# Eight conditioning chunks computed inside the first attention instead of in the output projection and feed-forward

## The reference, cut to what matters

```python
# first block
proj = rms_norm(h, norm_mix) @ w_in                      # 3128 columns
h = h + concat([rwkv7_group(...), nsa_group(...)]) @ w_out
h = h + (silu(rms_norm(h, norm_ffn) @ w_gate) * (rms_norm(h, norm_ffn) @ w_up)) @ w_down
# second block, for l in range(2)
mod_x = silu(c) @ w_ada[l] + b_ada[l]                    # 9 x 1024 modulation values
mod_c = silu(c_ctx) @ w_ada[l] + b_ada[l]
h_x = _half_ffn(...); h_c = _half_ffn(...)               # use mod_x, mod_c, from here on
...
```

## Time and profile before

| | |
|---|---|
| median of 3 runs | 2290.67 us (2289.95 to 2290.98) |
| the profiled execution | 2294.01 us, of which the span 2292.6 us |
| PE busy | 2161.4 us (94% of the span) |
| DVE, ACT, POOL busy | 1078.5, 772.7, 51.8 us |
| chain of work that ended last, by engine | PE 84%, DVE 7%, ACT 5%, DMA 2% |
| granted TensorE clock, mean | 0.962 of full |
| first attention | about 231 to 276 us of the span |
| output projection, norm, feed-forward of the first block | about 276 to 547 us |

### The profile page before, as it was taken

The page is one execution under the profiler, slowest core; times in us unless marked ns, Lnnn a source line. Parts: engine busy times, 40 slices in busy tenths (PEclk is TensorE's granted clock), DMA queues, the critical chain, the costliest instruction groups (busy, mean ns, idle before and its releaser), DMA issues.

```text
span 2292.6 us, 40371 instructions
## 1 busy us (share of the span) xinstructions
PE 2161.4 (94%) x17742; PEld 1845.1 (80%) x17742; DVE 1078.5 (47%) x1613; ACT 772.7 (34%) x1094; POOL 51.8 (2%) x58
## 2 busy tenths in 40 slices
PE   7987789998999999998899999999999999999998
PEld 7886589997888788785578888887888887768997
DVE  5654555456333333557563333345333335765554
ACT  5321434344221222324632222223222323364443
POOL 0000020000000000031000000000000000200000
PEclk9998689998999999999999999999999999999999
DMA  7526146654345444531023232232223225304543
GB/s 274 194 78 254 42 184 231 256 193 148 129 161 213 188 170 176 159 95 56 1 92 129 69 124 92 77 110 87 91 93 111 86 78 137 113 1 147 177 176 106
DMA packets 56635, 303.70 MB, mean 132 GB/s; under 512 B 13728, under 2 KB 17184, under 8 KB 27552
## 3 DMA queue, kind: packets, MB, share of 16 engines
q1 hardware_dynamic: 56480, 301.40, 37.0%
HBM read 300.33 MB, written 1.05 MB: 131 GB/s over the span
## 4 chain that ended last, share of the span: by engine, by line
PE 84%; DVE 7%; ACT 5%; DMA 2%; issue 2%; SPq 0%; ACTq 0%; DVEq 0%
PE ps L448 22%; PE ps L449 21%; PE ps L450 21%; PE ps L548 3%; PE ps L549 3%; PE ps L552 3%; DVE w_lo L435 3%; PE ps L477 3%; ACT w_hi L429 2%; PE ps L1559 1%; DVE mx L1892 1%; ACT ee L1839 1%; DMA raw<-in_w_gu 1%; PE ps L1809 1%; PE ps L1787 1%
## 5 line engine op out<-in xcount | busy, mean ns | idle before, releaser
L448 PE MATMUL ps<-a_hi,w_hi 128*128 128x512 f32 (+1 forms) x1992 | 688.7, 346 | 12.2 <-DVE w_lo L435 12.0
L449 PE MATMUL ps<-a_lo,w_hi 128*128 128x512 f32 (+1 forms) x1992 | 681.0, 342 | 0.0
L450 PE MATMUL ps<-a_hi,w_lo 128*128 128x512 f32 (+1 forms) x1992 | 680.4, 342 | 0.0
L435 DVE TENSOR_TENSOR w_lo<-raw,w_hi 128x2048 fp32r<-128x2048 f32 (+2 forms) x231 | 471.2, 2043 | 380.5 <-ACT w_hi L429 380.1
L429 ACT ACTIVATE w_hi<-raw 128x2048 fp32r<-128x2048 f32 (+2 forms) x229 | 391.8, 1717 | 375.7 <-PE ps L450 117.5
L448 PEld LDWEIGHTS ps<-a_hi,w_hi 128*128 128x128 f32 x1992 | 380.7, 191 | 60.1 <-DVE w_lo L435 13.2
L450 PEld LDWEIGHTS ps<-a_hi,w_lo 128*128 128x128 f32 x1992 | 380.8, 191 | 42.4
L449 PEld LDWEIGHTS ps<-a_lo,w_hi 128*128 128x128 f32 x1992 | 381.1, 191 | 40.8
L448 PE MATMUL ps<-ff_hi,w_hi 128*128 128x512 f32 (+1 forms) x880 | 309.7, 352 | 7.0 <-DVE w_lo L435 7.0
L449 PE MATMUL ps<-ff_lo,w_hi 128*128 128x512 f32 (+1 forms) x880 | 306.5, 348 | 0.0
L450 PE MATMUL ps<-ff_hi,w_lo 128*128 128x512 f32 (+1 forms) x880 | 306.2, 348 | 0.0
(11 more groups left out here) (351 smaller groups left out, 1807.8 us busy)
## 6 DMA issues: line engine op xcount, KB each, us to landing
raw<-in_w_gu SPq DMA_DIRECT2D x110, 1024.0 KB, 4.8
raw<-in_w_ada SPq DMA_DIRECT2D x72, 1024.0 KB, 6.5
raw<-in_w_dn SPq DMA_DIRECT2D x80, 704.0 KB, 4.0
raw<-in_w_in SPq DMA_DIRECT2D x26, 1024.0 KB, 5.2
raw<-in_w_out SPq DMA_DIRECT2D x12, 1024.0 KB, 4.8
direct<-in_w_cmp SPq DMA_DIRECT2D x4, 1024.0 KB, 7.2
h<-in_x SPq DMA_DIRECT2D x2, 1024.0 KB, 7.1
nb<-in_rpb SPq DMA_DIRECT2D x32, 64.0 KB, 6.6
```

Source lines behind the costliest of these rows:

```text
L435: nc.vector.tensor_tensor(w_lo[slot][:, cols], raw[b][:, cols], w_hi[slot][:, cols].bitcast(F32), ALU.subtract).then_inc(lo_ready if done ...
L448: nc.tensor.matmul(banks[m], w1, a1, start=start and k == 0, stop=False)
L449: nc.tensor.matmul(banks[m], w1, a2, start=False, stop=False)
L450: last = nc.tensor.matmul(banks[m], w2, a1, start=False, stop=stop and k == pr.kt - 1)
```

## The change

In the plan, `w_out` has no conditioning chunk any more, the two halves of `w_gu` have 3 and 4 (before: 4 and 5), and the first half of `w_dn` has one (before: 3). EARLY is 28, so that eight more chunks are loaded ahead of `w_out`. PE multiplies one of them at each t = 3 to 10 of the first attention, after the scores, into columns 256 to 383 of the output bank whose pairs are being made: two chunks a bank, in four batches. DVE drains three batches at t = 5, 7 and 9, ahead of the pair's own subtraction, and the fourth in `w_out` after the second chunk's additions. At odd t PE waits first for `at_olo`, which tells that the bank's former pair and the batch beside it have been taken out.

```diff
@@ -178,8 +178,8 @@
 
 
 ADA = N_MOD * KT // 2
-BATCHES = [(0, 5, 3), (5, 7, 3), (12, 8, 6)]
-EARLY = 20
+BATCHES = [(0, 5, 3, 0), (5, 7, 3, 0), (12, 8, 6, 0)] + [(20 + 2 * o, 2, 6 + o % 2, S) for o in range(4)]
+EARLY = 28
 IN_TILES = (12, 4, 6, 0, 2, 8, 10, 18, 14, 16, 20, 22)
 IN_SHIFTED = 7
 IN2 = (4, 5, 6, 3, 2, 1, 0)
@@ -232,10 +232,10 @@
 
     add("w_in", 12, KT, 2, S, "proj1")
     add("w_tail", 1, KT, 1, S, "tail1")
-    add("w_out", 4, KT, 2, S, "res", ada_at=range(4))
+    add("w_out", 4, KT, 2, S, "res")
     for half in range(2):
-        add_gu("w_gu", S, half, ((0, 2, 4, 6), (0, 2, 4, 6, 8))[half])
-        add("w_dn", KT, FH, 1, S, "down", half * KT, ada_at=((1, 4, 7), ())[half])
+        add_gu("w_gu", S, half, ((1, 4, 7), (1, 4, 7, 10))[half])
+        add("w_dn", KT, FH, 1, S, "down", half * KT, ada_at=((3,), ())[half])
     for l in range(LAYERS):
         for half in range(2):
             add_gu(f"w_gu1_{l}", T2, half, range(FH - RING * (1 - half)) if l == 0 else ())
@@ -494,14 +494,14 @@
     def early_ada(pe, n=1):
         for _ in range(n):
             a = early[0]
-            first, _, bk = next(b for b in reversed(BATCHES) if b[0] <= a)
+            first, _, bk, o = next(b for b in reversed(BATCHES) if b[0] <= a)
             x = early_at + a
-            multiply_ada(pe, (x // RING, x % RING), ps[bk][:, 64 * (a - first):64 * (a - first + 1)])
+            multiply_ada(pe, (x // RING, x % RING), ps[bk][:, o + 64 * (a - first):o + 64 * (a - first + 1)])
             early[0] += 1
 
     def early_drain(dve, q):
-        a, n, bk = BATCHES[q]
-        drain_ada(dve, a, n, ps[bk][:, 0:64 * n], q + 1)
+        a, n, bk, o = BATCHES[q]
+        drain_ada(dve, a, n, ps[bk][:, o:o + 64 * n], q + 1)
 
     def stream_drain(dve, a):
         drain_ada(dve, a, 1, ps[6][:, 0:64], a - EARLY + len(BATCHES) + 1)
@@ -748,6 +748,8 @@
                 if m < pr.mt - 1 and pr.squares is not None and isinstance(i, int) and i == pr.n - 1:
                     last.then_inc(res_drained, 1)
             last.then_inc(chunk_drained, 1)
+            if pr.name == "w_out" and i == 1:
+                early_drain(dve, len(BATCHES) - 1)
             if pr.kind == "proj1":
                 dve_ahead(dve, i)
             if pr.squares is not None and not (isinstance(i, int) and i == pr.n - 1):
@@ -1817,6 +1819,10 @@
         for t in range(n + 3):
             if t < n:
                 scores(j0 + t, jobs[t])
+            if key == "first" and t >= 3:
+                if t % 2:
+                    wait(pe, at_olo, (j0 + t - 3) // 2 - 1)
+                early_ada(pe)
             if 2 <= t < n + 2:
                 turn(j0 + t - 2, jobs[t - 2])
             if t >= 3:
@@ -1912,6 +1918,8 @@
             if 4 <= t < n + 4 and t % 2:
                 j, x = j0 + t - 4, jobs[t - 4]
                 dve.wait_ge(at_ohi, j // 2 + 1)
+                if key == "first" and t < n + 2:
+                    early_drain(dve, 3 + j // 2)
                 c = slice(x.tok, x.tok + S)
                 V.tensor_tensor(a_lo[:, x.tile, c], o_cols(j // 2), a_hi[:, x.tile, c].bitcast(F32),
                                 ALU.subtract).then_inc(at_olo, 1)
```

## The result

The changed kernel takes 2269.6 us (median of 4 runs, 2265.8 to 2271.1) against 2290.7 us: the ratio is 0.9899, 95% interval 0.9887 to 0.9911. It is 21 us faster. The profiled execution took 2269.6 us (span 2268.2), 24.4 us of span less than the profiled one before, which lay 3.3 us above its own median.

The account below looks back on a forecast made before the run. The prediction took the attention to be a round of waits, with PE and buffers scarce in the products behind it. Savings of 19.3 us less 5.8 us in the attention gave -13.5 us: 2277.2 us, range 2268.5 to 2284.5.

Parts of the forecast that it names:

- The attention, +5.8 predicted: First attention: eight added chunks of 1.23 us, mostly at full clock, partly hidden in PE's holes, cost +5.8 us.
- Rival A: First attention: the chunks raise TensorE's granted clock, so their net cost is +0.1 us; 2271 us in all, chance 0.20.
- the row at 250 us: First attention, profile before: PE busy all the time yet granted 0.50; used as evidence against a clock rise.
- the link of 5.25 us: First attention: PE works without a hole from the turn at 257.06 to 262.31; a clock rise would save 2.6 us.
- the five holes of the earlier trace: First attention: PE's waits of 1.01, 1.05, 0.60, 2.50 and 1.05 us, against which the added chunks were priced.
- Step 1: `w_out` and the norm behind it: three chunks off the path and a wait of 2.12 us go, 8.4 us saved.
- The walk: New schedule of `w_out` followed from 289.4: last split ahead of the norm ends at 309.0, before at 317.4.
- rival C: `w_out`: its loads come late all the same and hold up the splits, saving 3.7 us, not 8.4; 2282 us, chance 0.07.
- Steps 2 to 4: Feed-forward: first half of `w_gu` saves 1.2 us, first half of `w_dn` 2.5, second half of `w_gu` 7.2.
- step 4: Second half of `w_gu`: an earlier load removes 4.4 us of waiting and 2.8 us of slow clock, 7.2 us saved.
- Rival B: First attention stays at half clock throughout, so the chunks cost 11.8 us, not 5.8; 2283 us, chance 0.14.
- rival D: Attention hides no chunk (18.0 us), waits in `w_out` and second half of `w_gu` survive; 2299 us, chance 0.04.

Follow-up runs that it names:

- experiments 1 to 3: Kernel before plus eight unused conditioning multiplies in the attention: 0.9985; one-column matmuls in their place: 1.0080; changed kernel with an eighth of its attention multiplies: 2276.6 us.
- experiment 2: Kernel before with eight one-column matmuls added at each t = 3 to 10 of the first attention; ratio to the kernel before 1.0080.
- experiment 8: Changed kernel with POOL's squares of the context held back until five chunks of `w_gu` are drained; ratio to the kernel before 0.9902.
- x12: The changed kernel itself, nothing altered, measured once more; 2270.9 us, ratio to the kernel before 0.9919.
- Experiment 7: Kernel before with one conditioning chunk moved within the second half of `w_gu` (places 2, 4, 6, 8, 10), no work removed; ratio 0.9971, 6.7 us faster.
- experiment 4: Changed kernel with each of the eight conditioning multiplies in the attention done twice; 2278.5 us, ratio to the kernel before 0.9942.

## Why the prediction was right or wrong, step by step

**The attention, +5.8 predicted, -3.0 measured: the step that failed.** I priced the chunks at full clock against the holes of the old timeline, and kept the other matmuls at the clock that the old timeline had. Both halves of this cannot hold. Rival A said the clock would rise, at a chance of 0.20, and I spoke against it with the row at 250 us, PE busy without a hole at 0.50. That row was evidence for the mixture of matmuls it has, not for a mixture with conditioning chunks in it; experiments 1 to 3 show that it is this ingredient that counts. The better row was there: the conditioning chunks in the trace before stood at full clock nearly everywhere. A smaller error is the price of a chunk at half clock: I used 2.25 us, and the one at 238.44 took 1.93.

Rival A's own sum (+0.1) was 3 us short as well. I halved the link of 5.25 us once, but the same link stands in the round before, and its clock was low too (246 to 254 us above). With both links halved its sum would be -2.5. From job 3 to job 7 the gain is 3.5 us, up to there nothing, and the tail is 0.5 us longer: -3.0. What holds the rounds now is DVE and ACT. There a cost that I had set to nothing appears, the drain at t = 5, now a link (chain in order of time, after):

```profile
253.22 0.28 ACT a_hi L1869
...
253.53 0.33 DVE rt L484
...
253.95 0.10 DVE mod L486
254.04 0.41 DVE a_lo L1924
254.45 0.61 DVE ss L1888
```

0.5 us of the chain. The slack that job 6 had came from PE's slow scores of job 7, for which DVE stood idle 1.69 us before 262.31, and it went with them. Of the five holes of the earlier trace rows the first two are gone, the hole of 2.50 us has become 0.82, the others are 0.90 (was 0.60) and 1.05 (as before), and there is a new one of 0.41 at 258.34; the loads and the `at_olo` wait hold up nobody in the attention, as said.

The Trainium skill (TensorE: Matmul & The Clock Gate, "Why this matters for your kernels") says that keeping PE busy brings the full clock, which I set against the row at 250 us. It gave the right sign here and is still not what the runs show: experiment 2 kept PE busy 96% of 70.6 us at half clock. The Trainium skill says of transposes (the same page, "Part 4: PE-mode transpose") that they do not count as busy in the same way. The kernel before does not contradict it, since its busy stretches of turns, scores and products stayed at 0.50, but no run here had transposes alone, so it is not tested.

**Step 1, `w_out`: -8.4 predicted, -7.3 measured.** The walk was right in its form. Counted from `w_out`'s first matmul, the last split ahead of the norm ended after 35.7 us before and ends after 28.4; the walk had 27.3. The missing 1.1 us lie in the splits on DVE, which I took at 2.29 from the earlier trace rows and which took 2.51, 2.70 and, for the last two together, 5.03: 0.2 + 0.4 + 0.45. The cause is POOL: with it held back (experiment 8) they take 2.29, 2.29 and 4.50, and from the first addition to `h` to the last split's end it is 19.6 us, against the walk's 19.4 (289.6 to 309.0). In `x12` POOL's last sum ends at 301.91, just as the last two splits begin, and these take 4.49. The load of the context now goes out 20 us earlier, and with it POOL's squares moved beside `w_out`. I had listed that load as one that does not come late, and never asked what it sets off when it comes early. The trace before had a sign of it: there POOL's squares began at 306.01, and the split beside them, at 310.62, took 2.51. That the third load and rival C's wait did not matter is seen at the same place: no idle time of PE over 0.2 us is left between the product chunks.

**Steps 2 to 4, the feed-forward: -10.9 predicted, -10.9 measured.** Four chunks fewer at 1.23, the hole of 3.24 us at the second half and its slow clock: gone as worked out. It holds part by part: the first half of `w_gu` is 1.1 us shorter (1.2 predicted), `w_dn` up to the second half 6.9 (2.5 + 4.4) and the second half 2.9 (2.8), so the sum is not luck. Experiment 7 confirms step 4 by itself, if not all of its 6.0 us in the profile. The wait of 0.60 us, of which I had counted nothing, went, and one of 0.36 us came at 384.89, where a conditioning chunk no longer covers a split.

**The rest, 0 predicted, -3.4 measured** (-1.48 before the attention, -1.96 behind 488 us). Nothing of the change is there. In the stretches ahead of the attention the granted clock and PE's idle time differ from profile to profile of the same code. The medians of the two kernels differ by 21.1 us and the spans of the profiles by 24.4, so most of this is likely the spread of single executions. Steps 1 to 4 as predicted and -3.0 in the attention would give -22.3; as measured they give -21.2 (with w_out's -7.3), which is the medians' difference.

Rival B (half clock throughout) did not come: the clock was 0.92. Experiment 2 is the kernel that shows it, with one-column matmuls in the chunks' place; rival D had no part of it: both waits went together.

## What to carry to other kernels

When work is moved into a stage where PE idles or runs at the lower clock, ask what the work does to the clock of everything else in that stage, and judge it by what clock this very kind of matmul had elsewhere, not by whether PE looks busy there now. When a load is freed earlier, follow it to the engine that waits for it, also an idle one like POOL: its work moves too, and may land beside what was undisturbed. And before moving much, look for the one chunk that stands in a bad place of a buffer ring: moving it within its own stage gave a third of this gain.

## What the runs showed of the hardware that I had not expected

- **A busy PE can stay at half clock.** 68.0 us busy of 70.6 with one-column matmuls: 0.50. 34.2 of 41.2 with the conditioning chunks: 0.92. An eighth of those chunks: 0.65, as without any.
- **The same code gets a different clock from one execution to the next.** The attention with its eight chunks took 41.2 to 44.7 us at 0.84 to 0.92 in four profiles. A difference of 3 us in one stretch of two profiles is no effect yet; it takes a second profile of each kernel, or a whole time with its interval.
- **POOL and DVE hinder each other in both directions.** A sum on POOL that takes 0.7 to 0.8 us takes 2.66 when it falls beside a split on DVE, and the split takes 2.5 to 2.7 instead of 2.29. The Trainium skill (SBUF — State Buffer, "SBUF: two separate sides") says that a GpSimd operation and a VectorE operation with two SBUF inputs lock the port pair that they share, each for its whole instruction. The trace agrees: the sum ends at 291.91, 0.6 us behind the split (288.80 to 291.31), as if it had stood until then and taken nearly its own 0.7; the split grew by 0.22 us, less than one operation of POOL. Here is POOL beside that split in the changed kernel (timeline):

```profile
288.55 0.61 POOL L2238 TENSOR_TENSOR nrm<-h 128x256 f32<-128x256 f32 x1
289.25 2.66 POOL L2243 TENSOR_TENSOR ctx_sq<-ctx_sq,nrm 128x256 f32<-128x256 f32 x1
```

- **PE can stall inside its own stream**, with no releaser in the profile; it did so five times, for 0.3 to 1.6 us, in an attention with 1264 matmul records in 51.8 us (experiment 4), and 2 to 7 times, for up to 2.9 us, ahead of the attention in every profile here. Each time it went on 1.2 to 1.6 us after a 16 KB transfer of the instruction queue had ended. With the chunks' matmuls doubled, nine such transfers fell in the attention where there had been six, and a sum of busy times has no term for that.
